# Four modulation items of the second layer moved from the opening to the first layer's choice of tokens

## What is computed

```python
for each layer:
    mod = silu(cond) @ mod_w + mod_b                     # (6 * D,), one row for each of the two groups of tokens
    sh1, sc1, g1, sh2, sc2, g2 = split(mod, 6)
    h = rms_norm(x, norm1_w) * (1 + sc1) + sh1
    proj = h @ w_in                                      # three mixers: FFT convolution, attention, short convolution
    x = x + g1 * (merged @ w_o)
    h2 = rms_norm(x, norm2_w) * (1 + sc2) + sh2
    aff = softmax(h2 @ router_w)
    gate, idx = top_k(aff.T, cap)                        # each of 16 experts chooses 16 + 64 tokens
    x = x + g2 * scatter_add(expert(h2[idx]) * gate)
```

## Time and profile before

| | |
|---|---|
| median of 3 runs | 2237.48 us (2230.22 to 2239.42) |
| the profiled execution | 2238.46 us; its span 2236.7 us |
| PE busy | 2143.8 us, 96% of the span |
| DVE busy | 1614.6 us, 72% |
| ACT busy | 1101.9 us, 49% |
| POOL busy | 166.7 us, 7% |
| mean granted clock of PE | 0.981 |
| DMA | 435.78 MB, mean 195 GB/s |

### The profile page before, as it was taken

The page is one execution under the profiler, slowest core; times in us unless marked ns, Lnnn a source line. Parts: engine busy times, 40 slices in busy tenths (PEclk is TensorE's granted clock), DMA queues, the critical chain, the costliest instruction groups (busy, mean ns, idle before and its releaser), DMA issues.

```text
span 2236.7 us, 35921 instructions
## 1 busy us (share of the span) xinstructions
PE 2143.8 (96%) x13512; PEld 1748.0 (78%) x13512; DVE 1614.6 (72%) x2401; ACT 1101.9 (49%) x1714; POOL 166.7 (7%) x180
## 2 busy tenths in 40 slices
PE   7998999999989999899998999999989999899999
PEld 2448999999657998566667999999765999666666
DVE  6867786754768554899998778663668664699997
ACT  4434544222712134788884444332451225588884
POOL 1010000000000100111110000000000110021110
PEclk8999999999998999999999999999999999899999
DMA  9782333222222522999994233221404431899996
GB/s 378 258 281 97 123 132 132 76 74 85 102 94 105 170 98 110 385 380 383 386 392 159 88 135 142 99 81 59 159 11 160 139 138 58 318 385 378 382 382 277
DMA packets 75727, 435.78 MB, mean 195 GB/s; under 512 B 8972, under 2 KB 9708, under 8 KB 34621
## 3 DMA queue, kind: packets, MB, share of 16 engines
q1 hardware_dynamic: 54336, 352.87, 40.9%
q0 software_dynamic: 18320, 72.28, 10.3%
q10 hardware_dynamic: 2926, 8.64, 1.1%
HBM read 384.92 MB, written 48.84 MB: 194 GB/s over the span
## 4 chain that ended last, share of the span: by engine, by line
PE 74%; DVE 8%; DMA 7%; ACT 4%; issue 4%; DVEq 3%; ACTq 0%; SPq 0%; POOL 0%; POOLq 0%
PE ps L691 28%; PE ps L924 13%; PE ps L1231 7%; PE ps L1257 4%; DMA front<-in_stream 4%; PE ps L1235 3%; PE ps L870 3%; PE ps L1261 2%; PE ps L989 2%; PE ps L796 2%; PE ps L884 1%; DVE back L2238 1%; ACT back_r L1329 1%; DMA front<-kspec 1%; DVE nb L2207 1%
## 5 line engine op out<-in xcount | busy, mean ns | idle before, releaser
L691 PE MATMUL ps<-front_r 128*128 128x320 f32 x3584 | 589.7, 311 | 0.9 <-DVE back_r L2304 0.8
L691 PEld LDWEIGHTS ps<-front_r 128*128 128x128 f32 x3584 | 542.1, 189 | 2.2 <-DVE back_r L2304 1.4
L1329 ACT ACTIVATE front_r<-ring 128x1024 fp32r<-128x1024 f32 (+1 forms) x204 | 185.0, 907 | 328.1 <-PE ps L691 235.9
L1329 ACT ACTIVATE back<-ps 128x512 f32<-128x512 f32 (+5 forms) x200 | 98.0, 506 | 339.3 <-PE ps L691 174.1
L1790 DVE TENSOR_TENSOR front_r<-ring,front_r 128x1024 fp32r<-128x1024 f32 x100 | 122.3, 1223 | 151.9 <-ACT front_r L1329 150.8
L924 PE MATMUL ps<-back_r,front_r 128*128 128x320 f32 x1152 | 176.8, 309 | 0.0
L924 PEld LDWEIGHTS ps<-back_r,front_r 128*128 128x128 f32 x1152 | 170.9, 188 | 0.0
L2422 DVE TENSOR_TENSOR back_r<-front,back_r 128x1024 fp32r<-128x1024 f32 x128 | 153.3, 1218 | 5.1 <-ACT back_r L1329 3.6
L1231 PE MATMUL ps<-back_r 128*80 128x512 f32 x384 | 152.3, 397 | 3.7 <-ACT back_r L1329 3.7
L1231 PE MATMUL ps<-back_r,front_r 128*80 128x512 f32 x384 | 152.3, 396 | 0.0
L691 PE MATMUL ps<-back_r,front_r 128*128 128x320 f32 x640 | 147.6, 312 | 0.0
(11 more groups left out here) (311 smaller groups left out, 3730.1 us busy)
## 6 DMA issues: line engine op xcount, KB each, us to landing
ring<-in_stream SPq DMA_DIRECT2D x186, 1024.0 KB, 6.2
front<-in_stream SPq DMA_DIRECT2D x80, 1024.0 KB, 24.0
back<-in_stream SPq DMA_DIRECT2D x48, 1024.0 KB, 23.9
gates<-back SPq DMA_DIRECT2D x24, 640.0 KB, 3.1
back<-gates POOLq DMA_DIRECT2D x48, 320.0 KB, 3.3
kspec<-back POOLq DMA_DIRECT2D x20, 512.0 KB, 6.2
front<-kspec POOLq DMA_DIRECT2D x4, 2048.0 KB, 10.4
rows<-front ACTq DMA_DIRECT2D x10, 520.0 KB, 2.7
```

Of the source, the lines that this page charges most:

```text
L691: mm = pe.matmul(tokh(b)[:, c0:c1], w(wp)[:, k, :], src(hp, k)[:, c0:c1], start=first, stop=last)
L1329: return act.activation(o, i, ACT.Copy)
```

## The change

Layer 0 makes eight items at its choice of tokens instead of four (`LATE`), so the opening makes 25 instead of 29: two in each of the steps 0 and 1, one in each of the steps 2 to 19. The items keep their order, so each one made from step 3 on is an earlier one than before, the convolution of layer 0 makes 25 to 29, and the choice 30 to 37. Items 30 and 31 belong to `sc1` of layer 1, so the scale vector of layer 1's first norm is made by DVE at the end of layer 0's experts and no longer in its merge.

```diff
-MODS, LATE = DEPTH * N_MOD, ((5, 4), (6, 4))
+MODS, LATE = DEPTH * N_MOD, ((5, 8), (6, 4))
 EARLY = MODS - sum(sum(n) for n in LATE)
...
         def step_mods(n):
 
-            if n < 3:
-                return 3 + 2 * n, 4 + 2 * n
-            return (6 + n,) if n < 17 else (2 * n - 11, 2 * n - 10)
+            return (3 + 2 * n, 4 + 2 * n) if n < 2 else (5 + n,)
...
                     if n == 0:
                         branch_lo(2)
-                    if n == 12:
-
-                        dve.wait_ge(modcol_read, late_mods(l, 0)[-1] + 1)
-                        weighed_scale(1, l)
+                    if n == 12 and l == 1:
+
+                        dve.wait_ge(modcol_read, late_mods(1, 0)[-1] + 1)
+                        weighed_scale(1, 1)
...
                 if l + 1 < DEPTH:
+                    dve.wait_ge(modcol_read, late_mods(l, 1)[-1] + 1)
+                    weighed_scale(1, 0)
                     split(l + 1, 0)
                     split(l + 1, 1)
```

## The result

The changed kernel took 2241.53 us (median of 17 runs, 2236.89 to 2245.08). The kernel before, run beside it, took 2232.75 us (median of 17, 2229.61 to 2240.08). The medians lie 8.8 us apart. The ratio over all runs is 1.003 (6.7 us), with a 95% interval from 1.0021 to 1.004: a loss of 0.2 to 0.4%, within the half per cent that the forecast called no change.

The account below looks back on a forecast made before the run. PE bounds nearly everywhere, DMA also in the opening and experts, both finishing the experts together. Opening −5.9 plus the larger choice side, +7.9, gave +2.0 us on the 2237.48 median: 2239.5 us, range 2235 to 2243.

Parts of the forecast that it names:

- Steps 17 to 19: Opening: each step loses one item, which PE alone closes; −4.1 us, bounds −3.2 and −4.4.
- Step 2: Opening: without its second item the next taps start earlier, half clock taking part back; −1.6 us, bounds 0 and −2.4.
- Behind step 19: End of the opening: a spectrum's store lands sooner with fewer ring loads beside it; −0.2 us, bounds 0 and −0.4.
- Convolution and scale vector: Layer 0: convolution still makes five items; the moved scale vector is covered by DVE's wait for PE; 0 us.
- Choice, SP's queue: Layer 0's choice and experts: four more loads delay landings from the fourth expert item on; +7.9 us, bounds 3.5 and 10.0.
- room of 2.1 us: DMA queue before the experts: idle capacity, between 1.6 and 2.7 us, taken off the four loads' 10.0 us.
- Choice, PE's side: Layer 0's choice: four more items, partly filling PE's idle 3.90 us; +3.5 us, bounds 2.7 to 6.2, not summed.
- The signs: Trace marks named beforehand: 6.1 us steps, longer ACT waits, landings 2 to 3 us longer, experts' stage near 290 us.
- rival A: Experts' stage: DMA has slack, so only PE's 3.5 us is lost; −2.4 us, 2235; chance 0.23.
- B: Choice: first gather starves beside more loads and experts start late; +4.1 us, 2241.6; chance 0.13.
- C: Choice: added items fit PE's idle time and their loads the queue's room; −5.4 us, 2232; chance 0.09.
- D: Opening: steps don't shrink, as DVE's wait for a spectrum's store replaces the item; +6.1 us, 2243.6; chance 0.05.

Follow-up runs that it names:

- after: The changed kernel itself, eight items at layer 0's choice of tokens, against the kernel before: 2241.53 us, ratio 1.003.
- after_again: The same changed kernel, run and profiled a second time on another occasion: 2240.27 us, ratio 1.0024 to the kernel before.
- open_only: The changed kernel without the four items added at the choice, neither loaded nor computed: 2229.90 us, ratio 0.999 to the kernel before.
- conv9: The changed kernel with its four added items moved from the choice to layer 0's convolution, which makes nine: 2230.21 us, ratio 0.9986 to the kernel before.
- loads_pool: The changed kernel with the four added items loaded but not computed, GpSimd giving their slots back: 2240.74 us, ratio 1.0023 to the kernel before.
- loads_only: The changed kernel with the four added items loaded but not computed, PE waiting for each landing: 2239.98 us, ratio 1.0027 to the kernel before.
- items_more: The changed kernel with the four added items computed from data already in SBUF, nothing loaded for them: 2238.60 us, ratio 1.0007 to the kernel before.
- before_behind: The kernel before with all four items of the choice made behind the turn of the places, both layers: 2240.47 us, ratio 1.003 to the kernel before.
- after_filled: The changed kernel plus one full-array matmul beside each item of the choice's second group: 2238.43 us, ratio 1.0026 to the kernel before.

## Why the prediction held, and where it was off

The sign, the size within half a per cent and the mechanism held: the opening shortens by less than the experts' queue lengthens. The forecast of 2239.5 lies 2.0 us from the 2241.5 measured, but part of that nearness is luck. It stood on a median of three runs, 2237.48; 17 runs of before gave 2232.75. As a difference I forecast +2.0 us and the ratios say +5.4 and +6.7, over an interval of +2.7 to +8.9.

- *Steps 17 to 19, −4.1:* measured 3 × 1.36 = −4.1. Right.
- *Step 2, −1.6:* measured −0.5 in after and −1.5 in after_again, both inside the bounds. In after_again the taps behind the step start at 50.86, for the 50.9 reckoned. Half clock then takes its part in both traces: the taps of steps 3 and 4 are 6.50 (58.46 − 51.96) and 6.45 us apart, and were 5.46, since the two matmuls ahead of the second take 1.91 us for 1.02. So of 2.40 us gained at step 3 after_again keeps 1.41 at step 4, and after keeps 0.26 of 1.30 (58.72 before). What the sum did not have is that in after, with the same program, half clock came already with step 2's one item.
- *Behind step 19, −0.2:* 171.12 − 143.98 = 27.14 us from those taps to the norm, before 28.76; less step 19's own 1.36 that is −0.26. Right. The opening in sum: −5.0 in after, −6.0 in after_again, for the −5.9 forecast; −3.2 and −4.4 in the totals of open_only and conv9.
- *Convolution and scale vector, 0:* right. DVE has the vector at 1191.52, and still waits 0.39 us for PE at 1194.34 (1.01 in the earlier trace rows). Its cover has shrunk, but it is there.
- *Choice, SP's queue, +7.9:* the step that was mis-sized. The four loads measured 307.58 − 297.91 = 9.7 us in loads_pool, and 10.6 in loads_only; after less conv9 is 10.0 to 10.6. That is the bound with no room at all. My room of 2.1 us was read from GB/s. The share in the same rows was 1.05 and 0.98 at 346 and 235 GB/s: with gathers in flight the engines were taken, however few bytes they moved. Only the row with share 0.52 had room, 0.48 × 2 = 1.0 us, and 10.0 − 1.0 = 9.0 would have been the number. I had named that share as the ground for the bound and then not used it.
- *Choice, PE's side, +3.5:* mis-sized too. In the traces it is 9.3 us at the start (21.57 − 12.25) and 7.5 at the end (items_more less conv9), above my bound of 6.2; in the totals 1.3 to 3.8. The bound took 2.52 us for an item at half clock, the matmuls and ACT's copy; in a row it is 2.81, since the turn of the last item's columns stands between. I chose near the full clock because the second item of the pair had run at 1.48 us. Six in a row all ran at 1.93, while in before_behind four in a row ran at 1.07: the clock at this place changes with the kernel. As the sum takes the larger side only, this did not reach the result.

**The signs.** Seen: 6.1 us from taps to taps, groups of 16 at the choice and no idle time before the turn of the rows, layer 1 within 1.1 us. Not seen: ACT waited 1.84 us for the fourth expert item, not 3 or more; loads issued in the window at 1110 land after 26.4 us, not 2 to 3 above 28.7; PE's wait for the sums' rows fell to 0.36; the stage stayed at 285.3 and did not near 290. I tied all four to PE being on time and the queue late. PE was as late as the queue, so the lateness had nothing to be measured against. In loads_pool, where PE's work ends as in before, three of them are there: ACT waits 4.62 us for the fourth expert item, PE 1.11 us for the sums' rows, and the stage takes 307.58 − 17.04 = 290.5 us. By the sign that I had named, an unchanged length, rival A would have been declared true. It is loads_pool and after_filled that refute it.

*Rival A* (DMA has slack): refuted; without PE's delay the loss stays. *B* (the gather starves): the first gather was issued at 883.06, took 8.3 us, and PE did not wait for it. *C*: refuted. *D*: steps 17 to 19 shrank.

**On the rate.** One window shows what the queue does in the stage. Layer 0's experts, in conv9 and then in loads_pool, the columns as before:

```profile
905.00:1165.00 260.00, 258.80 (x1244) 169.10 (x1243) 248.74 (x285) 223.20 (x287) 42.45 (x27) 1.00 1.02 387
```

```profile
905.00:1165.00 260.00, 255.37 (x1215) 166.64 (x1214) 242.39 (x275) 219.47 (x281) 42.11 (x27) 0.99 1.02 387
```

Before and after also have 387 GB/s and a share of 1.02. Four loads of 1.05 MB at this mean are 10.8 us, and measured are 9.7 to 10.6. The prediction's 2.5 us between two landings gives 10.0. Either prices them to within a tenth; what was wrong was the room taken off. The Trainium skill, "DMA: Bandwidth & Descriptors", section "Where 436 GB/s comes from", binds a load by HBM at about 358 GB/s for a core, which it gets as half of a stack's 716 GB/s, for two cores. Here one core runs, and the mean of 387 over 260 us, and 422 to 438 in single windows, lie above it; the measurement decides.

What stays open: how far PE's side alone costs time on average (two sets of runs disagree), what sets the gather's time, and whether the slots' later release or the gather alone makes the order behind the turn slower.

## What to carry to other kernels

When a stage is bound by two resources at once, price a moved step in each and look for the larger; the trace of the changed kernel can then show only one of them, and an experiment that moves each alone is needed to see the other. Room in a DMA queue is read from its busy share, not from GB/s, and a load's price is about its bytes over the mean rate of the saturated stage. And profile a kernel twice before a difference of one or two us is explained: step 2 gained 0.5 us in one trace of the changed kernel and 1.5 in the other. Before moving loads, list the stages by DMA share: the same four items cost 10 us with the experts at a share of 1.02, and nothing that could be measured in the convolution at 0.3 to 0.6.

## What was not expected of the hardware

PE ran for 6 us without a gap (888 to 894 in after: busy 2.00 of 2.00 us, three times) at a granted clock of 0.50. The Trainium skill, "TensorE: Matmul & The Clock Gate", section "Part 1: The HAM clock gate", holds that activity releases the throttle. By the busy share of these rows that did not happen. At full clock items in a row are 1.66 us apart (before_behind, 881.36 to 883.02), at half clock 2.81, so six of them would have taken up to 6 × 1.15 = 6.9 us less, an estimate that leaves out the waits for loads. With one matmul on the full array beside each item (after_filled) the granted clock was 1.00 from 884 to 892.

With gathers in flight the DMA engines are taken without moving much: 260 GB/s at a share of 1.09, and 235 at 0.98. And starting the first gather 2.75 us earlier brought nothing, since it then took 9.81 us for 6.97; why is open.
